# A two-layer decoder kernel: the shared expert's down product moved into the expert loop, and the routing's operations put in another order

## What the kernel computes

```python
scores = sigmoid(xt @ router_w)                       # 256 x 64
choice = scores + router_b                            # best 4 of 8 groups, then the best 8 experts
top_w  = top_w / sum(top_w) * 2.5
h      = silu(xb @ w1[e]) * (xb @ w3[e])              # for each expert e and its tokens xb
acc    = acc.at[tok].add((h @ w2[e]) * weight)
shared = (silu(xt @ s_w1) * (xt @ s_w3)) @ s_w2       # the shared expert; the last product is its down product
out    = acc + shared
```

## Time and profile before

| | |
|---|---|
| Median of 3 runs | 1538.94 us (1537.63 to 1539.3) |
| Profiled execution, its own time | 1537.95 us |
| Span of the profile | 1536.2 us |
| PE busy | 1368.2 us (89%) |
| DVE, ACT, POOL busy | 550.0, 442.4, 203.0 us |
| Read from HBM | 514.10 MB, 335 GB/s over the span |
| Chain that ended last | PE 58%, DMA 25%, DVE 7% |

### The profile page before, as it was taken

One profiled execution on the slowest core, in us unless ns is written; L12 is line 12 of the kernel. 1 busy time (PEld: TensorE's weight loads), 2 busy tenths in 40 slices (PEclk: granted clock), 3 DMA queues, 4 the chain that ended last, 5 costly groups with the idle time before them and its releaser, 6 DMA issues.

```text
span 1536.2 us, 33031 instructions
## 1 busy us (share of the span) xinstructions
PE 1368.2 (89%) x12029; PEld 888.6 (58%) x12030; DVE 550.0 (36%) x1217; ACT 442.4 (29%) x872; POOL 203.0 (13%) x651
## 2 busy tenths in 40 slices
PE   4798787999899998998699996889998999899986
PEld 2796456555455554454399984765554555455543
DVE  1434657322222322232443425473232323222333
ACT  2332344222222221222434433332221222222222
POOL 7001010211111111111000000012111111111110
PEclk9898798999999999999889998989999999999998
DMA  9999981799979999999985540526999899989995
GB/s 307 382 376 350 352 311 70 307 422 422 422 327 422 422 422 422 422 422 423 377 258 176 182 137 28 198 91 278 421 422 422 336 422 422 422 341 422 422 422 233
DMA packets 113757, 515.86 MB, mean 336 GB/s; under 512 B 10120, under 2 KB 47120, under 8 KB 63792
## 3 DMA queue, kind: packets, MB, share of 16 engines
q1 hardware_dynamic: 109920, 509.64, 83.3%
q0 software_dynamic: 2368, 3.36, 0.8%
q10 hardware_dynamic: 1424, 2.23, 0.4%
HBM read 514.10 MB, written 1.09 MB: 335 GB/s over the span
## 4 chain that ended last, share of the span: by engine, by line
PE 58%; DMA 25%; DVE 7%; SPq 3%; ACT 3%; issue 3%; ACTq 1%; DVEq 0%
DMA ring<-in_exp_w_dram 23%; PE bank L790 20%; PE bank L948 17%; PE bank L969 4%; PE bank L951 4%; PE bank L893 3%; PE bank L924 3%; PE bank L766 3%; DMA ring<-in_da_w_in_dram 2%; PE bank L975 2%; SPq L317 2%; SPq L351 1%; PE bank L883 1%; DVE ring_r L1155 1%; DVE arena L1287 1%
## 5 line engine op out<-in xcount | busy, mean ns | idle before, releaser
L948 PE MATMUL bank<-ring,arena 128*64 128x512 f32 x1120 | 279.0, 618 | 33.8 <-DMA ring<-in_exp_w_dram 33.8
L948 PEld LDWEIGHTS bank<-ring,arena 128*64 128x64 f32 x1120 | 91.4, 141 | 191.4 <-issue 190.5
L924 PEld LDWEIGHTS bank<-arena 128*128 128x128 bf16 x3264 | 142.1, 98 | 55.5 <-issue 54.9
L893 PE MATMUL bank<-arena_r 128*128 128x512 f32 x560 | 161.5, 418 | 3.0 <-DVE arena_r L1299 3.0
L924 PE MATMUL bank<-arena 128*128 128x64 bf16 (+1 forms) x3264 | 151.8, 207 | 0.0
L1299 DVE TENSOR_TENSOR arena_r<-bank,arena_r 128x512 fp32r<-128x512 f32 x136 | 94.0, 692 | 154.1 <-ACT arena_r L648 154.1
L641 ACT ACTIVATE arena<-bank 128x256 f32<-128x256 f32 (+1 forms) x68 | 22.6, 333 | 427.4 <-PE bank L948 309.7
L951 PE MATMUL bank<-ring,arena 128*32 128x256 f32 x2112 | 131.2, 390 | 11.8 <-ACT arena L636 11.8
L648 ACT CAST arena_r<-bank 128x512 fp32r<-128x512 f32 x136 | 79.6, 585 | 189.6 <-PE bank L969 124.9
L893 PEld LDWEIGHTS bank<-arena_r 128*128 128x128 f32 x560 | 94.6, 188 | 60.6 <-issue 47.4
L790 PE MATMUL bank<-HH_r,ring_r 128*128 128x256 f32 x448 | 128.7, 287 | 0.0
(11 more groups left out here) (257 smaller groups left out, 1878.4 us busy)
## 6 DMA issues: line engine op xcount, KB each, us to landing
ring<-in_exp_w_dram SPq DMA_DIRECT2D x384, 1024.0 KB, 16.4
ring<-in_ada_w_dram SPq DMA_DIRECT2D x48, 1024.0 KB, 11.0
ring<-in_ret_w_in_dram SPq DMA_DIRECT2D x24, 1024.0 KB, 9.5
ring<-in_da_w_in_dram SPq DMA_DIRECT2D x12, 1024.0 KB, 13.5
ring<-in_ret_w_out_dram SPq DMA_DIRECT2D x8, 1024.0 KB, 4.9
ring<-in_sh_w_dram SPq DMA_DIRECT2D x6, 1024.0 KB, 7.3
ring<-in_da_w_out_dram SPq DMA_DIRECT2D x4, 1024.0 KB, 8.9
mods<-mod_dram POOLq DMA_DIRECT2D x4, 512.0 KB, 6.0
```

The source lines that it names most:

```text
L893: ins = nc.tensor.matmul(banks[4 + NH * tc + hf][:, :], S[:, P * tc:P * tc + P], y[:, r, 512 * hf:512 * hf + 512], start=False, stop=(last ...
L924: ins = nc.tensor.matmul(banks[2 - 2 * half][:, P * kk:P * kk + 2 * W], parts[:, tc, r, P * (4 * half + kk):P * (4 * half + kk + 1)], Pg[: ...
L948: ins = nc.tensor.matmul(banks[1][W * i:W * i + W, :], xg[:, k, W * i:W * i + W], w13[j][:, k, :, :], start=(k == 0), stop=(k == KD - 1))
```

## The change

The shared w2 leaves the ring: it goes by a DMA of its own to `sh_w2_tile`, a part of `arena`, issued in SP's queue ahead of the load of expert tile 10. The pads go too, so the ring holds two expert tiles more at that time. The down product stands between the third and the fourth step of the expert loop (`SHARED_AT = 3`), and PE's loop is therefore two loops, of 3 and of 13 steps. In its old place there are four matmuls with a zero `S` that open banks 4 to 7; `y` is no longer set to zero.

The routing's order changes: the count matmuls stand before the whole up product, the placing ones before its second half; DVE makes `low_part("shared", l, 1)` before the rest of `h`, takes the rest and part 2 in two halves (one per 128 tokens, `tc`), puts the ranking directly behind the choice, and the weights behind the ranking; the second half of the rest, part 2 and the shared activation come after `route_ready`. ACT makes part 1 in two halves, each behind its half of the rest. POOL makes the pass limits once the experts are chosen, and in each pass the one-hots before the copies of the weights, with a new semaphore `wsel_ready` for which PE waits before L932.

```diff
-    order += [("shared", 0, i) for i in range(3)] + [("pad",)]
+    order += [("shared", 0, i) for i in range(2)]
...
+                    if n == MOE0[l] + RING - 2:
+                        sp.wait_ge(sh_gate_up, l + 1)
+                        sp.dma_start(sh_w2_tile, sh_w2[l].rearrange("(p b) n -> p b n", b=2)).then_inc(sh_w2_in, 16)
...
-                pool.wait_ge(sh_up, l + 1)
+                pool.wait_ge(chosen_ready, l + 1)
...
-                nc.gpsimd.memset(y.bitcast(F32), 0.0).then_inc(u["bank0_read"], 1)
...
-                act.wait_ge(rest_ready, l + 1)
-                nc.scalar.copy(parts[:, :, 1, :], h).then_inc(part_mid, 1)
+                for tc in range(TC):
+                    act.wait_ge(rest_ready, TC * l + tc + 1)
+                    nc.scalar.copy(parts[:, tc, 1, :], h[:, tc, :]).then_inc(part_mid, 1)
                 act.wait_ge(sh_up, l + 1)
                 nc.scalar.activation(sg, banks[0][:, :], ACT.Silu).then_inc(sh_silu, 1)
                 release(2)
-                act.wait_ge(sh_down, l + 1)
-                release(MOE0[l] - where["shared", l, 2])
...
+                def shared_down():
+                    pe.wait_ge(sh_w2_in, 16 * (l + 1))
+                    for tc in range(TC):
+                        for hf in range(NH):
+                            for b in range(2):
+                                nc.tensor.matmul(banks[4 + NH * tc + hf][:, :], shT[:, b, P * tc:P * tc + P],
+                                                 sh_w2_tile[:, b, 512 * hf:512 * hf + 512], start=False, stop=False,
+                                                 skip_group_check=True)
...
+                pe.wait_ge(u["S_ready"], 1)
+                pe.wait_ge(u["bank0_read"], 1)
+                for bank in banks[4:8]:
+                    nc.tensor.matmul(bank[:, :], S[:, 0:P], y[:, 0, 0:512], start=True, stop=False, skip_group_check=True)
+                pe.wait_ge(route_ready, l + 1)
+                pe.wait_ge(sh_ready, l + 1)
                 pe.wait_ge(parts_ready, l + 1)
-                pe.wait_ge(route_ready, l + 1)
...
+                            pe.wait_ge(u["wsel_ready"], g + 1)
...
+                with pe.Fori(0, SHARED_AT) as it:
+                    steps_of(it)
+                shared_down()
+                with pe.Fori(SHARED_AT, STEPS) as it:
+                    steps_of(it)
...
+                rest_part(1)
+                low_rest_part(0)
+                dve.wait_ge(sh_silu, l + 1)
+                nc.vector.tensor_tensor(shT, sg.rearrange("p (b t) -> p b t", b=2),
+                                        banks[1][:, :].rearrange("p (b t) -> p b t", b=2), ALU.mult).then_inc(sh_ready, 1)
+                low_rest_part(1).then_inc(parts_ready, 1)
```

More of the change, by code:

```diff
@@ L54, in plan_stream @@
     order += [("mix_in", 1, i) for i in range(24)] + [("mix_out", 1, i) for i in range(8)]
-    order += [("shared", 1, i) for i in range(3)] + [("pad",)]
+    order += [("shared", 1, i) for i in range(2)]
     moe[1] = len(order)
@@ L75, in trunk @@
     order, MOE0 = plan_stream()
-    where = {key: n for n, key in enumerate(order) if key[0] != "pad"}
-    loads = [sum(1 for m in range(n % RING, n + 1, RING) if order[m][0] != "pad") for n in range(len(order))]
+    where = {key: n for n, key in enumerate(order)}
+    loads = [n // RING + 1 for n in range(len(order))]
     assert all(MOE0[l] % 2 == 0 for l in range(DEPTH))
@@ L309, in load @@
             def load(n, src):
-                out_rows = order[n][0] in ("mix_out", "ada") or order[n][0:3:2] == ("shared", 2)
+                out_rows = order[n][0] in ("mix_out", "ada")
                 sp.dma_start(tile_out(n) if out_rows else tile_in(n), src).then_inc(landed[n % RING], 16)
@@ L510, in _ @@
                             ins.then_inc(u["onehot_ready"], 1)
+                            pool.wait_ge(weights_ready, l + 1)
+                            for j in range(2):
+                                ins = nc.gpsimd.tensor_copy(wsel_of[:, 6 * j:6 * j + 6], wparts_of[:, bass.ds(pair[j] * 6, 6)])
+                            ins.then_inc(u["wsel_ready"], 1)
                 if l == 0:
@@ L853, in moe @@
                     ws = [w.rearrange("p k (m b) -> p k b m", b=2) for w in parts_of(("shared", l, i))]
+                    if i == 1:
+                        pe.wait_ge(chosen_ready, l + 1)
+                        nc.tensor.matmul(banks[3][:, 0:E], upper[:, :], mb[:, 0, :], start=True, stop=True)
+                        nc.tensor.matmul(banks[3][:, E:2 * E], ones[:, :], mb[:, 0, :], start=True, stop=False)
+                        nc.tensor.matmul(banks[3][:, E:2 * E], upper[:, :], mb[:, 1, :], start=False, stop=True)
+                        for tc in range(TC):
+                            nc.tensor.matmul(banks[3][0:E, 2 * E:3 * E], ones[:, 0:E], mb[:, tc, :],
+                                             start=(tc == 0), stop=(tc == TC - 1))
+                        for tc in range(TC):
+                            ins = nc.tensor.matmul(banks[3][0:E, 3 * E:3 * E + 1], mb[:, tc, :], ones[:, 0:1],
+                                                   start=(tc == 0), stop=(tc == TC - 1))
+                        ins.then_inc(ranks_done, 1)
@@ L863, in moe @@
-                            for tc in range(TC):
-                                ins = nc.tensor.matmul(banks[3][0:E, 3 * E:3 * E + 1], mb[:, tc, :], ones[:, 0:1],
-                                                       start=(tc == 0), stop=(tc == TC - 1))
-                            ins.then_inc(ranks_done, 1)
+                            pe.wait_ge(at_rank_ready, l + 1)
+                            nc.tensor.matmul(banks[3][0:1, 4 * E:5 * E], expert_id[:, 0:1], at_rank, start=True, stop=True)
```

81 lines of the change are left out of this document (31 added, 50 removed).

## The result

The median rose from 1537.77 us (1535.51 to 1539.3, 14 runs) to **1540.95 us** (1539.46 to 1544.06, 14 runs): ratio 1.0024, interval 1.0016 to 1.0032. The forecast was 1536.6, the range 1531.5 to 1541.0. The time lies at the range's upper end: slower, where a little faster was forecast. The profiled execution took 1540.36 us with a span of 1538.6, against 1537.95 and 1536.2.

A forecast was written before the change was run, and what follows sets the result against it. TensorE lines and the expert weights' DMA were taken to fill the chain. Start 2 x 1.5 less 0.7 for the product gives 2.3 us off 1537.95, 1535.6; the median, 1.0 above, is forecast 1536.6, range 1531.5 to 1541.0.

The forecast's parts named there:

- Left of the earlier start: 3.1 - 1.6 = 1.5 us in each layer: Loop start: gather 3.1 us earlier, less 1.6 for the low clock; 1.5 per layer, from 0.7 to 3.6, carried on.
- Entering the loop: Behind parts_ready, PE's loop entry and register load in the open: taken as 0.6 us, between 0.1 and 2.84.
- The low clock: First gather after PE's 4.2 us idle wait: slow matmuls cost 1.6 us, between 0 and 2.4.
- rival B: Loop start no earlier, since loop entry takes up to 2.8 us and the clock drops; 1539, chance 0.20.
- The product in step 3, layer 0: Expert loop, layer 0: the product's 7.13 us hidden by 9.7 us of waits and a clock drop that goes.
- the 1.36 us of the fall in step 4: Layer 0, step 4: a clock drop, 8.41 - 7.05, expected to go and counted in the product's cover.
- 0.7 lost by the product: Expert loop, layer 1: 6.5 us of cover in steps 4 and 5 against 7.13, so 0.7 us lost.
- the code of the second loop: Split expert loop: fetching the second loop's code once per layer costs 0 to 3 us, taken as 0.
- signs of being wrong: Table load before the second copy, PE starting over 1 us from 273.2, or later, longer tile waits in steps 3 to 6.
- the chances for "within": Whole time within about 0.2% (3.1 us) of before: 0.20 of the forecast and 0.17 of B, given as 0.38.
- Rival C: Step 3, layer 1: late refills run the transfers dry, product not paid back; 1543.1, or 1550.2 in both layers; chance 0.15.
- Rival A: Loop start: clock kept, 5.5 us less (1533.4); table load hidden too, 4.5 per layer, 8.3 less (1530.6); chance 0.25.

The follow-up runs named there:

- experiment 6: The changed kernel with PE's wait for parts_ready moved into each pass, behind its register loads; 1540.08 us, ratio 1.0011 to before.
- experiment 3: The changed kernel with 20 matmuls of zeros behind the four opening ones, keeping PE busy through the idle stretch; 1537.7 us, ratio 0.9998 to before.
- Experiments 7 and 10: The changed kernel with 20 matmuls of zeros and the Silu before ACT's second copy, with and without the parts_ready wait inside the pass; 1538.64 and 1538.3 us.
- experiment 4: The changed kernel with the down product between the eighth and ninth step (SHARED_AT = 8); 1546.47 us, ratio 1.005 to before.
- 3 + 13: The kernel before, with only PE's expert loop cut into loops of 3 and 13 steps; 1539.53 us, ratio 1.001.
- experiment 11: The changed kernel with 20 matmuls of zeros, the Silu first, and the product between the first and second step; 1549.06 us, ratio 1.0065 to before.
- experiment 5: The changed kernel with ACT's Silu and its table load ahead of its second copy; 1537.74 us, ratio 0.9992 to before.
- experiment 12: The changed kernel with the Silu first and 12 matmuls of zeros keeping PE busy; 1535.52 us, ratio 0.9983 to before.
- 8 + 8: The kernel before, with only PE's expert loop cut into two loops of 8 steps; 1542.06 us, ratio 1.0023.

## Why the prediction was wrong

**The start: the step that failed is "Left of the earlier start: 3.1 - 1.6 = 1.5 us in each layer".** `parts_ready` came 17.3 behind the turning, predicted 16.9 (272.6 - 255.72); 0.36 of the 0.4 are there already at `route_ready` (11.24, predicted 10.88). Entering the loop cost 1.50 and 1.29 us, taken as 0.6; experiment 6 shows that 1.0 of it is what lies between the two places of the wait, the entry into the loops and their loads of registers, in the open. The gather's lead was therefore 1.62 and 1.87 us for 3.1. The low clock cost 1.5 and 2.2, taken as 1.6, and inside its bounds of 0 to 2.4; experiment 3 shows that it is the clock, since zeros on PE remove it. So 0.10 of gain and 0.37 of loss, for 1.5 twice. This is rival B's mechanism, and B's middle, a start that gives about nothing, was the right price for it. B's total of 1539 still lacks what made the kernel slower: the fall, the code and the stretch between the loops, below.

**What the start is worth.** The sum carried its gain to the end one to one. Experiments 7 and 10 show that 2.5 us per layer come back as nothing, in layer 0 by two falls. In layer 0 a start 1.5 us earlier did arrive in full (experiment 3), but only because no fall stood in step 5. The two effects are of one size, and the sum had only one of them.

**The product in step 3, layer 0: hidden, as predicted,** and the cover was there: waits of 2.52 and 2.66 us gone, landing unchanged. What the step did not see is that cover taken from one wait makes the next one longer, and that the clock falls in long waits. I had subtracted the 1.36 us of the fall in step 4 as a gain. It was replaced by one of 1.70 in step 5, behind which there is no cover. Experiment 3 has the same wait there without a fall and experiment 4 the old waits with the old fall, and neither has this loss.

**Layer 1, taken as 0.7 lost by the product and 1.5 won by the start, measured 1.35 lost.** The second step that failed is the code of the second loop, "0 to 3 us, taken as 0": the tiles go back by 1.3 us right behind its first packet and stay there, where those ahead of it landed 0.1 earlier than before's. The cut alone gives 0.7 (3 + 13); why after has more stays open. The product itself is covered in full: PE waits for a tile in step 5. Nor does the start's 0.37 show in the landings. The prediction looked for a stall of PE, and none came; it is the tiles that pay. The trace of before had shown it: tile 15 of layer 0 lands 1.5 us late right behind such a packet.

**Between the loops,** a term that the sum didn't have: +0.99. The projections, which the change doesn't touch, take 41.04 and 5.50 us in the chain above; before, the same stood as

```profile
953.90 39.85 PE bank L790 x168
...
1007.25 5.06 PE bank L790 x24
```

which is 1.6 longer after, in the same instructions; 0.6 of it is won back elsewhere in the stretch. The clock is lower in a part of them. Across all kernels the distance between the loop's end and the next turning is 263.2 to 265.2 us, with 263.60 before. The eight kernels with 263.2 to 263.6 have one stretch of 20.5 us at 1.2 GHz behind the loop; five, after among them, have two of 6.8 there and 263.9 to 264.9; experiment 6 has one of 17.1 and 265.2. What decides between them stays open.

**Together:** the fall 1.70, the code 1.30 and the stretch between the loops 0.99 make 4.0; tiles that landed 0.37 and 0.12 earlier take 0.5 off, 0.3 isn't traced further. The sum had -3.0 for the start, +0.7 for the product and nothing for these three. That the time still lies inside the range is luck. Two of the prediction's own signs of being wrong came: PE starts 1.3 us away from the predicted place behind the turning, and the wait of step 5 is longer than before. Two slips had no effect: the load of the shared w2 is issued at 267.08, ahead of the Silu and not behind it, and the chances for "within" add up to 0.37, not 0.38.

**Rival C** was refuted at step 3 by the landings and confirmed at step 1 (experiment 11), where its condition, a queue shorter than PE's delay, holds. Its addition for the loop's code was right in kind. **Rival A's** part on the table load is right: hidden, it brings 1.46 us to the gather (experiment 5). Its price is not: with the clock kept as well it had 8.3 us less, and experiment 12, which has both, starts the gather 3.1 us earlier for A's 4.5 and is 2.6 us below before. The Trainium skill ("ScalarE: Activation LUTs", "What ACT_TABLE_LOAD costs") adds a drain of about 1380 ns to the load; the trace has the Silu 0.02 us behind the end of the load, so no drain is seen here, and the sum's 1.28 was the right price.

## What to carry to other kernels

Work that fills one wait lengthens the next, so follow it to the last wait in front of the stretch where the engine itself is the bound: what is lost there stays, and what is lost before is paid by the transfers. A matmul chain that is started earlier, out of an idle engine, begins with the clock low and with the loop's register loads in the open; price both before counting the lead. Here the table load taken off the path and a few matmuls of zeros that end before the gather can start were worth more than a wait moved behind the register loads. An earlier start is worth something only if no fall stands in the last wait ahead of such a stretch, and these traces don't say how to arrange that. A loop that is cut in two brings its code a second time through a stream that may be full, and early in such a stream, while its queue is short, added work starves it.

## What the runs showed of the hardware

- **Falls of the clock in waits.** Over 14 traces, the 99 waits for a tile of about 0.5 to 1.4 us (as the rows measure them) had no fall, two of the six of 1.7 to 2.3 us had one, of the 121 of 2.4 to 2.9 us 76, and all three above 3; the matmuls behind one of the 76 took 1.3 to 1.7 us longer. They don't look like chance: with the same start, before and its 3 + 13 cut have theirs at the same places, 135, 292, 380 and 442 us behind the turning in layer 0, and 142, 299 and 456 in layer 1. The Trainium skill ("TensorE: Matmul & The Clock Gate", "The HAM clock gate") says that the moment differs from run to run; here it moved with the kernel's timing and repeated with it, as far as single profiled executions can show.
- **Twelve matmuls of zeros** (2.89 us of PE), with the Silu first, are enough to have the gather at 2.85 us in both layers. Without them it took 4.12 and 2.85 (experiment 5), in after 4.36 and 5.08.
- **32 KB of code** put every later landing in a full stream of 1 MB tiles back by up to 1.5 us (8 + 8, layer 0; nothing in layer 0 at step 3), though they are 0.03 of 12.64 MB in 30 us.
